# Two transformer blocks on one core: GpSimd's subtractions to VectorE, residual rows written earlier, conditioning sums placed elsewhere, a third load buffer

## The reference, cut to what matters

```python
# block "o"
ada = silu(c) @ w_ada + b_ada                      # 6 x 1024: shift, scale, gate, twice
h = rmsnorm(x, g_mix) * (1 + scale1) + shift1
proj = h @ w_in                                    # dilated + neighbourhood attention, two gates
x = x + gate1 * (merged @ w_out)
h2 = rmsnorm(x, g_ffn) * (1 + scale2) + shift2
u = depthwise_conv_seq(h2 @ w_up, conv_w, conv_b)  # width 3 over the tokens
x = x + gate2 * ((gelu(u_gate) * u_val) @ w_down)
x = rmsnorm(x, g_final)
# layers "0" and "1", each of three sub-blocks: swiglu, token mixer, swiglu
mod = silu(c_2) @ ada_w[l] + ada_b[l]              # 9 x 1024: shift, scale, gate of each sub-block
h = rms_norm(x, g_pre) * (1 + scale) + shift
x = x + res_w * (1 + gate) * rms_norm(y, g_post)   # y: the sub-block's output, res_w 0.5, 1, 0.5
```

## Time and profile before

| | |
|---|---|
| time, three runs | 1850.04, 1851.20, 1852.59 us; median 1851.2 |
| the profiled execution | 1852.85 us, of which the span from the first to the last instruction is 1851.0 |
| granted TensorE clock, mean | 0.975 of 2.4 GHz |
| busy: TensorE, VectorE, ScalarE, GpSimd | 93%, 68%, 46%, 3% |
| read from DRAM | 396 MB, 214 GB/s over the span |

### The profile page before, as it was taken

How to read it: one execution, slowest core, us unless ns; L and a number is a source line. 1 busy time by engine, 2 the same in 40 slices (tenths; PEclk the granted TensorE clock), 3 DMA queues, 4 the chain that set the end, 5 groups by cost and what they waited for, 6 DMA issues and landing times.

```text
span 1851.0 us, 29566 instructions
## 1 busy us (share of the span) xinstructions
PE 1726.7 (93%) x12340; PEld 1599.4 (86%) x12340; DVE 1260.8 (68%) x1812; ACT 859.2 (46%) x1188; POOL 58.8 (3%) x46
## 2 busy tenths in 40 slices
PE   1999969997899989999979999999989999979998
PEld 1999869986899879989969997899878989969996
DVE  6677779986777656666657774777566666757644
ACT  3555355542533354665453334533354665453333
POOL 1000010001000000000010001000000000010000
PEclk9999979999899989999989999999999999989999
DMA  8776755578477854545456776477754545456563
GB/s 343 270 263 218 212 195 192 197 265 295 156 274 273 261 193 152 226 150 193 175 143 251 273 244 244 173 273 276 260 193 174 212 160 198 167 143 244 182 174 134
DMA packets 70933, 398.92 MB, mean 216 GB/s; under 512 B 8208, under 2 KB 8464, under 8 KB 36112
## 3 DMA queue, kind: packets, MB, share of 16 engines
q1 hardware_dynamic: 67536, 386.58, 59.6%
q0 software_dynamic: 2832, 8.95, 1.4%
q10 hardware_dynamic: 432, 1.50, 0.2%
HBM read 395.92 MB, written 1.08 MB: 214 GB/s over the span
## 4 chain that ended last, share of the span: by engine, by line
PE 73%; DMA 11%; ACT 5%; DVE 5%; DVEq 2%; issue 1%; ACTq 1%; SPq 1%
PE lin L429 20%; PE lin L430 20%; PE lin L431 20%; PE att L542 7%; DMA raw<-in_w 6%; ACT hi L779 3%; DMA ada_w<-in_ada 3%; DVE lo L1093 2%; PE att L628 2%; DMA rows<-post_gain 1%; PE pt L655 1%; PE att L678 1%; DVE ada_w L1100 1%; DMA ra<-rows 1%; DVEq L1275 1%
## 5 line engine op out<-in xcount | busy, mean ns | idle before, releaser
L1093 DVE TENSOR_TENSOR lo<-raw,hi 128x2048 fp32r<-128x2048 f32 x261 | 598.0, 2291 | 339.1 <-ACT hi L779 338.8
L429 PE MATMUL lin<-h_hi,hi 128*128 128x256 f32 x2720 | 782.0, 288 | 30.5 <-DVE h_lo L1157 30.5
L430 PE MATMUL lin<-h_lo,hi 128*128 128x256 f32 x2720 | 774.4, 285 | 0.0
L431 PE MATMUL lin<-h_hi,lo 128*128 128x256 f32 x2720 | 774.1, 285 | 0.0
L779 ACT ACTIVATE hi<-raw 128x2048 fp32r<-128x2048 f32 x269 | 513.4, 1909 | 294.4 <-DMA raw<-in_w 195.2
L429 PEld LDWEIGHTS lin<-h_hi,hi 128*128 128x128 f32 x2720 | 525.9, 193 | 34.8 <-issue 34.6
L430 PEld LDWEIGHTS lin<-h_lo,hi 128*128 128x128 f32 x2720 | 526.1, 193 | 1.1 <-issue 1.0
L431 PEld LDWEIGHTS lin<-h_hi,lo 128*128 128x128 f32 x2720 | 525.5, 193 | 0.0
L1100 DVE CUSTOM_DVE_ANT_0 ada_w<-ada_w,cs 128x1024 f32<-128x1024 f32 x179 | 225.1, 1260 | 35.1 <-DMA ada_w<-in_ada 25.6
L959 ACT ACTIVATE work<-lin 128x256 f32<-128x256 f32 x88 | 33.8, 385 | 303.7 <-PE lin L431 303.7
L542 PE MATMUL att<-hi,act_hi 128*128 128x512 f32 x440 | 139.3, 397 | 3.5 <-DVE lo L1093 3.5
(11 more groups left out here) (245 smaller groups left out, 1791.6 us busy)
## 6 DMA issues: line engine op xcount, KB each, us to landing
raw<-in_w SPq DMA_DIRECT2D x269, 1024.0 KB, 4.8
ada_w<-in_ada SPq DMA_DIRECT2D x179, 512.0 KB, 5.0
ada_s<-in_ada SPq DMA_DIRECT2D x13, 512.0 KB, 15.1
bias<-in_bias POOLq DMA_DIRECT2D x16, 256.0 KB, 4.4
ffn_row<-rows POOLq DMA_DIRECT2D x5, 512.0 KB, 8.9
x<-in_x ACTq DMA_DIRECT2D x1, 1024.0 KB, 6.8
cs<-in_cond SPq DMA_DIRECT2D x2, 512.0 KB, 6.3
dcon<-in_dcon SPq DMA_DIRECT2D x1, 1024.0 KB, 10.0
```

The lines of the kernel that those rows point to most:

```text
L429: mm(out, w_hi, a_hi, start=start, stop=False, skip_group_check=skip)
L430: mm(out, w_hi, a_lo, start=False, stop=False, skip_group_check=skip)
L431: return mm(out, w_lo, a_hi, start=False, stop=stop, skip_group_check=skip)
L1093: tt(lo[c % SPLIT][:], raw[:, c % RAW, :], hi[c % SPLIT][:].bitcast(F32), ALU.subtract).then_inc(*s_lo.up(c))
```

## The change

1. `RAW` is 3: a chunk's load waits for the `lo` of the chunk three before. The activated conditions share one buffer `cs` (the second is loaded by GpSimd's queue when the first block's sums are made, and its Silu comes at the head of o.down), and `rs`, `lat_hi`, `lat_lo` and four gates lie in tiles that are free at the time.
2. GpSimd subtracts nothing; VectorE makes every `lo`.
3. The columns for the rows are made earlier: "out" in slot 12 of the mixing, "down" ahead of o.down, "post1" in slot 8 of the mixing. The broadcast of "out" waits until the dilated heads' values are used, that of "post1" for the last score, since the row lies in their tiles.
4. The sums move: none in the stages "out"; in the mixing of o up to two a slot, in o.up 8 (at every second chunk from up.1 to up.15), in o.down 16 (two at each of eight chunks), in the layers' down0 8 and mixing 20.
5. `rest_of_stage`: products of half 0, then, if normed, the first product of half 1, the update of half 0, the second product; the update of half 1 goes in two halves, and its square in the next norm too.
6. `log_exp` stands ahead of the splits of the stage "down" or "out".
7. At the start chunk 0 is loaded ahead of the last eight sums' rows, its `lo` is made behind sum 12, VectorE no longer waits for `par` ahead of the sums, and makes the `lo` of chunk 1 behind the first `modulated`.

```diff
-RAW = 2
+RAW = 3
...
-    at += list(range(5, 25)) + [26, 26, 27, 27, 28, 28] + [36, 42]
-    at += [c for c in range(AT["o.down.0"] + 2, AT["o.down.0"] + 12) for _ in range(2)]
+    at += list(range(4, 21)) + [20, 21, 21, 22, 23, 24, 25]
+    b = AT["o.up.0"]
+    at += [b + 3 + 2 * i for i in range(8)]
+    at += [c for c in range(AT["o.down.0"] + 2, AT["o.down.0"] + 10) for _ in range(2)]
...
-        at += [b + 3 + i for i in range(20)] + [b + 24 + i for i in range(10)]
+        at += [b + 3 + i for i in range(20)] + [b + 24 + i for i in range(8)]
         s = AT[f"{l}.moba.k1"] + 2
-        at += [s + i for i in range(2, 12)] + [s + i for i in range(16, 22)]
-        o = AT[f"{l}.out.0"] + 2
-        at += [o, o + 1]
+        at += [s + i for i in range(2, 13)] + [s + i for i in range(16, 25)]
...
-BY_POOL = [AT["o.dil.k0"], AT["o.up.1"]] + [AT[f"{l}.{n}"] for l in range(LAYERS) for n in ("up0.1", "moba.k0", "up2.1")]
...
             for h in range(ADA_START):
-                if h == ADA_START - 2:
+                if h == 8:
                     load_chunk(0)
                 load_ada(h)
...
-                    eng.wait_ge(*s_cond_in.at(0))
-                    eng.dma_start(cs[:, 1, :], d["cond"][:, D:2 * D].to_broadcast([P, D])).then_inc(
-                        *s_cond_in.up(1, n=16))
...
                 eng.wait_ge(*s_row_out.at(tag))
+                if tag == "out":
+                    eng.wait_ge(*s_pv.at(("o", HEADS - 1)))
+                if tag[2:] == "post1":
+                    eng.wait_ge(*s_scored.at((tag[0], 3 * HEADS - 1)))
                 eng.dma_start(row_of(tag), rows[i:i + 1, :].to_broadcast([P, D])).then_inc(*s_row_in.up(tag, n=16))
...
             turned_row("out", mod[:, 16:24])
-            split("o.up.1")
+            eng.wait_ge(*s_ada_used.at(ADA_ONCE - 1))
+            eng.dma_start(cs[:], d["cond"][:, D:2 * D].to_broadcast([P, D])).then_inc(*s_cond_b_in.up(1, n=16))
             turned_row("down", mod[:, 40:48])
...
+            def norm_of_x(tag, by):
+
+                eng.wait_ge(*s_x.at((by, 0)))
+                act(two(by_token(work_all)[:, 0, :]), two(x[:, 0, :]), ACT.Square, accum_out=total[:, 0, 0:1])
+                root(tag, 0, 0, eps[:, 0:1])
+                for half in range(2):
+                    eng.wait_ge(*s_x.at((by, 1, half)))
+                    act(work[2 + half], x[:, 1, half * 512:(half + 1) * 512], ACT.Square,
+                        accum_out=total[:, 1, half:half + 1])
+                    if half == 0:
+                        half_done(1)
+                root(tag, 1, 1, total_of_half[:, 1:2])
...
+            eng.wait_ge(*s_cond_b_in.at(1))
+            act(cs[:], cs[:], ACT.Silu).then_inc(*s_silu.up(1))
+            log_exp()
             down("o.down")
-            log_exp()
...
+                eng.wait_ge(*s_row_in.at(tag))
+                times(0, 1)
+                times(0, 0)
+                if normed:
+                    times(1, 1)
+                    plus(0)
+                    times(1, 0)
+                else:
+                    plus(0)
+                    times(1, 1)
+                    times(1, 0)
+                plus(1)
...
-            eng.wait_ge(*s_par_in.at("par"))
             eng.wait_ge(*s_silu.at(0))
             for h in range(ADA_START):
                 ada_one(h)
-                if h == ADA_START - 2:
+                if h == 12:
                     split(0)
+            eng.wait_ge(*s_par_in.at("par"))
...
             modulated("norm1", 0)
+            split(1)
             split(2)
...
-            mixing("o", ONCE_HEADS, "dil.v0", ONCE_SLOTS, {})
+            mixing("o", ONCE_HEADS, "dil.v0", ONCE_SLOTS, {12: [lambda: gate_of(16, "out")]})
+            shift_and_gain("o.1", 24, par[:, PCOL["b_ada"]][:, 24:40], par[:, PCOL["g_ffn"]], gain[:, 8:16])
...
+            gate_of(40, "down")
             for k in range(FD - 1):
...
-                    0: [lambda: rotate_moba(l, "q1")], 1: [lambda: rotate_moba(l, "k1")],
+                    0: [lambda: rotate_moba(l, "q1")], 1: [lambda: rotate_moba(l, "k1")], 8: [lambda: layer_post(l, 1)],
...
-                layer_post(l, 1)
+                layer_gain(l, 2)
```

More of the change, by code:

```diff
@@ L1008, in _ @@
                     *s_gated.up(("o.up", k)))
+            eng.wait_ge(*s_cond_b_in.at(1))
+            act(cs[:], cs[:], ACT.Silu).then_inc(*s_silu.up(1))
+            log_exp()
             down("o.down")
-            log_exp()
-            for a in range(2):
-                eng.wait_ge(*s_x.at(("down", a)))
-                norm_factor("norm3", a, two(x[:, a, :]))
+            norm_of_x("norm3", "down")
             for l in map(str, range(LAYERS)):
@@ L1184, in rest_of_stage @@
                         eng.wait_ge(*s_r.at((tag, a)))
-                    halves = 2 if tag == "1.post2" and a else 1
-                    for half in range(halves):
-                        part = slice(half * 512, half * 512 + D // halves)
+                    for half in range(1 + a):
+                        part = slice(half * 512, half * 512 + D // (1 + a))
                         if normed:
@@ L1425, in _ @@
                 split(c)
+                if k == 0:
+                    eng.wait_ge(*s_silu.at(1))
                 ada(AT[f"o.down.{k}"])
[L1427 to L1428 removed]
             layer_gain("0", 0)
@@ L1433, in _ @@
                 eng.wait_ge(*s_r.at(("norm3", a)))
-                stt(x[:, a, :], x[:, a, :], factor[:, a:a + 1], last_row[:], ALU.mult, ALU.mult).then_inc(
-                    *s_x.up(("norm3", a)))
+                for half in range(1 + a):
+                    part = slice(half * 512, half * 512 + D // (1 + a))
+                    stt(x[:, a, part], x[:, a, part], factor[:, a:a + 1], last_row[:, part], ALU.mult, ALU.mult).then_inc(
+                        *s_x.up(("norm3", a, half) if a else ("norm3", a)))
             scaled_x("0.pre0", flat_f)
```

125 lines of the change are left out of this document (50 added, 75 removed).

## The result

In the first comparison the changed kernel took 1802.55 us (median of 4 runs, 1801.51 to 1803.37), the kernel before 1851.83 us (4 runs, 1850.04 to 1852.59). The ratio is 0.9735, with a 95% interval of 0.9718 to 0.9752. The forecast was 1801, in a range of 1789 to 1817.

What follows compares the result with a forecast made beforehand. TensorE, busy 93% of the span, was taken as the bound, so only its idle time could go. Terms summed to -50.6 us from 1852.9, giving 1802.3, or 1800.6 by the median; forecast 1801, range 1789 to 1817.

Steps and rivals of the forecast that it cites:

- the normed ends: Ends of 0.down0, 0.out, 0.down2, 1.down0 and 1.out: 10.9 us each (10 to 11.5) from last to next first weight product.
- o.out: End of o.out: without sums and with row and gain earlier, 23.6 us becomes 9.4, -14.1.
- the start: Before the first weight product: no GpSimd subtraction beside VectorE, chunk 1 sooner; -4.3 us (-2.5 to -5).
- o.down: Fewer sums per stage, three raw buffers: -3.5 us inside; its end from 23.5 to 13.7 us, -9.8.
- The rows of 0.out and 1.out: Ends of 0.out and 1.out: rows asked for earlier end VectorE's wait, 19.3 and 19.2 us become 10.9 each, -16.7.
- Rival 5: Waits in GpSimd's in-order queue keep the rows late, 0.out and 1.out stay at 19: 1818 us; 0.12 together with Rival 3.
- Rival 2: VectorE becomes the bound in the first block, at o.up and o.down's scatter: 1807 to 1809 us; chance 0.2.
- o.up: Eight sums instead of two make VectorE lag and TensorE stop: +2.3 us (0 to +5).
- at nothing: Slot 8's drains, second condition's load, Silu and table loads, four more sums per mixing: covered by other work, no cost.
- Rival 1: Ends become so short that TensorE's clock holds: 9 us less, 1792 us; chance 0.15.
- Rival 3: GpSimd's subtraction was cover VectorE needs at seven ends: 2.3 us each, 1817 us; 0.12 together with Rival 5.
- Rival 4: Sums' loads land late behind three raw loads and hold up VectorE: slower, 1871 us; chance 0.03.

Runs made afterwards that it cites:

- e3: Changed kernel with the gate row of o.out and the post-norm rows of 0.out and 1.out written behind their mixing again; span 1829.9 us.
- e7: Changed kernel with the second token half's square taken whole, not in two halves, at all seven ends; span 1795.6 us.
- e12: Changed kernel with ScalarE's table load behind the last hi copy again at all stage ends; span 1802.1 us.
- e5: Changed kernel with the old order at normed ends: both products of a token half, its update, then the other half; span 1805.2 us.
- e1: Changed kernel with two raw weight buffers again instead of three; span 1808.5 us.
- e4: Changed kernel with conditioning sums back in the out stages, 0.down0 and 1.down0, rows still early; span 1805.1 us.
- e2: Changed kernel with the removed subtractions back on GpSimd, one in the start and one at each of seven stage ends; span 1800.5 us.
- e6: Changed kernel with o.down's gate row formed and scattered after o.up's sixteenth chunk, not at o.down's head; span 1786.3 us.
- e8: Changed kernel with o.up's eight sums moved into the first mixing and o.down's gate row scattered early in o.up; span 1787.7 us.
- e9: Changed kernel again, unaltered; median of four runs 1794.81 us, ratio 0.9702 to the kernel before.

## Why the prediction was right, and where it was not

**The total** came out within 2 us of the first comparison's median (1801 against 1802.55), partly because errors cancelled: the normed ends, o.out and the start gave 5.7 us more than forecast, o.down 5.1 less, and the first mixing lost 1.2. Span to span it was 51.6 us against a sum of 50.6. That the forecast is so near is in part luck.

- *The rows of 0.out and 1.out*, -16.7: measured -18.0. The mechanism is shown by e3. Rival 5 has fallen: VectorE waits for no row in the out stages.
- *The normed ends*, 10.9 each: measured 9.6 to 10.2, so the five terms together were -25.1 and not -21.0. At 0.down2 the last factor came 6.8 us behind the stage's last product, where I had laid out 7.5; half of that miss lies ahead of the second post-norm factor (2.9 for 3.2), half behind it (3.9 for 4.3). From factor to first product it was the 3.3 us of the working. Two steps inside were wrong all the same: the halved square does not give its 0.7 us back (e7: some 0.4 less an end without it), and moving the table load gave nothing instead of 0.5 (e12). The order product, product, product, update gave 1.1 to 1.6 of the 1.72 us (e5), and the third buffer was the reason at 0.down0 and 1.down0 (e1).
- *o.out*, 9.4 and -14.1: measured 8.6 and -15.0. The step said that VectorE's products start late because it still sums. For the kernel before that is what the trace shows, by 3 us. But the row stood just behind the sums, hidden by them. Put back alone, the row costs 12.5 us (e3), the sums 4.3 (e4), two buffers 4.0 (e1) and GpSimd's subtraction 1.4 (e2). They add up to more than the 15.0, since each is hidden in part by the others. The prediction moved all four, and so met the size; it gave the third buffer no share in this term.
- *o.down*, -3.5 inside and -9.8 at the end: measured -1.5 and -6.7, the largest miss. The step that failed is "VectorE is free at 448.8": I let the scatter cost the stage 1.4 us and its end nothing. It cost VectorE a wait of 9.61 us, of which 3.3 were still there at the end. Without it both terms are met (e6: 61.8 and 13.6). Rival 2 named this place, but priced it at 3.5 us; e6 says 6.6.
- *o.up*, +2.3: measured +2.7, with periods of two chunks of 12.1 us in place of 11.5 from up.11 on. The count of the lag held: TensorE's stops there add up to 1.6 us, where 2 were forecast.
- *The start*, -4.3: measured -5.0; e2 shows 3.3 to 3.6 of it to be GpSimd's subtraction.
- *The first mixing*, nothing: measured +1.2. Two sums in one slot lie ahead of VectorE's merges at the first branch, and TensorE stops for 1.24 and 0.55 us. In e4, without a second sum there, it doesn't stop, and in e8, whose double slots lie earlier, for 0.21. "TensorE idles inside the mixings" was one of the prediction's own signs of being wrong, and in this mixing it came true: the term "at nothing" for the mixings' sums failed here, since busy time (158 of 245 us, and of another mixing) does not show what lies ahead of a merge.
- *0.down2 itself*, no term: measured -0.95 (62.71 to 61.76 us). The prediction says that outside the stretches only o.down has idle time; TensorE also stopped for 0.69 us in 0.down2 for a `lo`, and after the change it did not. No run isolates why.
- *The clock*, 0: some 1 us less in the first profile, some 8 us less in e9's. Rival 1 asked for ends so short that the clock holds. It held at more restarts in one run than in another, so the rival was true for some executions and not for others; e9's median, 1794.8, lies between it and the forecast.
- *Rival 3* (cover by GpSimd): true at the normed ends with 0.54 us of the 2.3 it was given. *Rival 4* (late loads): behind the start, VectorE waited for loads of sums in o.down alone, 9.61 us beside the scatter; in e6, without the scatter, it waited up to 2.48 us there and TensorE did not stop.

The Trainium skill's rule (page TensorE: Matmul & The Clock Gate, section HAM oscillation) that waits between bursts bring the throttle back agrees with both profiles in its direction. Whether an end as short as these restarts at the full clock no run here can foretell: 0.down0's did in both profiles, and those of 0.out, 0.down2 and 1.down0 did in e9 and not in the first, with the same idle time between dummy products and transposes (2.07, 1.92 and 1.92 us).

## What to carry to other kernels

Where two late things stand in front of the same wait, put each back alone before you credit either; before the change the one that ends last hides the other. Price a small scatter to DRAM by what its neighbours on the queues ask for in its 10 us, and place it in the stage that asks for least. An operation split in two for overlap pays only where its second input is late, so look whether the consumer ever waits for it.

## What the runs showed of the hardware

A write of 4 KB in single elements held up the other loads for some 10 us, wherever it was put (GpSimd's waits of 9.75, 10.91, 9.66 and 10.40 us in the changed kernel, e6, e8 and e12); in o.down the loads asked for in that time landed after it. Windows of the changed kernel during the write and behind it: 26 GB/s, then 320.

```profile
core 0: us, PE busy (x) PEld busy (x) DVE busy (x) ACT busy (x) POOL busy (x), PEclk, DMA share, GB/s
378.50:388.00 9.50, 9.50 (x42) 7.64 (x41) 6.06 (x8) 3.83 (x2) 1.06 (x2) 1.00 0.26 26
386.30:396.00 9.70, 9.18 (x40) 7.04 (x38) 1.84 (x3) 1.91 (x1) 1.06 (x2) 1.00 0.88 320
```

The same program, with the same 1.92 us of idle at 0.down2's end, restarted at a granted clock of 0.53 in one execution and of 1.00 in another; three such restarts made 7 us.
